# The last output projection as three rounded products, and the last expert loaded in smaller pieces

## The reference, cut to what matters

```python
mixed = jnp.concatenate([o_gla, o_att], axis=-1)     # o_gla and o_att end in a per-column gain
h = h + mixed @ w_out[l]                             # (256,1024) @ (1024,1024)
h = h + hier_moe(rms_norm_2(h, norm2_gain[l]), w_group[l], b_group[l], w_expert[l], b_expert[l],
                 w_gate[l], w_up[l], w_down[l])
return rms_norm_2(h, final_gain)
```

## Time and profile before

| | |
|---|---|
| median of 3 runs | 1330.17 us (1329.52 to 1331.28) |
| the profiled execution | 1329.42 us, its span 1327.6 us |
| PE busy | 966.9 us, 73% of the span |
| DVE, ACT, POOL busy | 451.8, 281.9, 41.8 us |
| mean DMA rate over the span | 350 GB/s, 464.45 MB |

### The profile page before, as it was taken

One profiled execution on the slowest core, in us unless ns is written; L12 is line 12 of the kernel. 1 busy time (PEld: TensorE's weight loads), 2 busy tenths in 40 slices (PEclk: granted clock), 3 DMA queues, 4 the chain that ended last, 5 costly groups with the idle time before them and its releaser, 6 DMA issues.

```text
span 1327.6 us, 30597 instructions
## 1 busy us (share of the span) xinstructions
PE 966.9 (73%) x13784; PEld 668.0 (50%) x13784; DVE 451.8 (34%) x1013; ACT 281.9 (21%) x632; POOL 41.8 (3%) x38
## 2 busy tenths in 40 slices
PE   9999999999999876466475746647574664757474
PEld 6998778888866433233243423324342432434242
DVE  4798776788844221111010211101021111102121
ACT  5655343738332100000000010000000000000001
POOL 0000201011120000000000000000000000000000
PEclk9999999999999988788787878878797978879798
DMA  9562455235494999999999999999999999999996
GB/s 329 164 246 82 150 190 190 99 112 203 175 429 177 400 433 431 427 430 433 428 431 438 429 429 435 428 429 431 436 430 434 431 429 428 431 433 432 429 426 270
DMA packets 56023, 464.45 MB, mean 350 GB/s; under 512 B 6250, under 2 KB 15268, under 8 KB 37924
## 3 DMA queue, kind: packets, MB, share of 16 engines
q1 hardware_dynamic: 55040, 460.81, 83.5%
q10 hardware_dynamic: 932, 2.92, 0.6%
HBM read 462.67 MB, written 1.05 MB: 349 GB/s over the span
## 4 chain that ended last, share of the span: by engine, by line
DMA 47%; PE 43%; DVE 6%; ACT 1%; issue 1%; SPq 1%; POOL 0%; POOLq 0%; DVEq 0%; ACTq 0%
DMA second_set<-in_w_up 41%; PE bank L2234 15%; PE bank L2877 9%; DMA ring<-in_w_up 5%; PE bank L2786 5%; PE bank L2769 3%; PE bank L2188 3%; PE bank L2212 2%; DVE ring_lo L1380 1%; PE bank L2282 1%; PE bank L2391 1%; PE bank L2299 1%; PE bank L2416 1%; DVE expert_area L2040 1%; DVE qk L1351 1%
## 5 line engine op out<-in xcount | busy, mean ns | idle before, releaser
L2890 PE MATMUL bank<-consts 128*32 128x32 f32 x52 | 8.0, 247 | 237.9 <-DMA second_set<-in_w_up 170.7
L2234 PE MATMUL bank<-ring_lo,xt_hi 128*128 128x512 f32 (+3 forms) x544 | 171.9, 383 | 0.2 <-DVE ring_lo L1380 0.2
L2786 PE MATMUL bank<-ring,consts 128*32 128x256 f32 x1952 | 118.7, 382 | 69.7 <-DVE consts L2043 41.0
L1266 ACT ACTIVATE expert_area<-bank 128x128 f32<-128x128 f32 x64 | 15.0, 275 | 656.4 <-PE bank L2877 577.6
L2040 DVE TENSOR_TENSOR expert_area<-expert_area,bank 128x128 f32<-128x128 f32 x64 | 22.9, 358 | 340.0 <-ACT expert_area L1266 340.0
L2890 PEld LDWEIGHTS bank<-consts 128*32 128x32 f32 x52 | 4.7, 138 | 245.9 <-DMA second_set<-in_w_up 176.9
L2786 PEld LDWEIGHTS bank<-ring,consts 128*32 128x32 f32 x1952 | 62.7, 109 | 121.8 <-issue 59.9
L2877 PE MATMUL bank<-second_set,expert_area 64*32 64x256 f32 x3328 | 119.4, 452 | 1.1 <-issue 1.1
L2877 PE MATMUL bank<-ring,expert_area 64*32 64x256 f32 x3328 | 118.8, 452 | 0.0
L2234 PEld LDWEIGHTS bank<-ring_lo,xt_hi 128*128 128x128 f32 x544 | 99.1, 188 | 18.4 <-issue 1.5
L2877 PEld LDWEIGHTS bank<-second_set,expert_area 64*32 64x32 f32 x3328 | 70.5, 127 | 44.6 <-issue 26.9
(11 more groups left out here) (351 smaller groups left out, 1400.5 us busy)
## 6 DMA issues: line engine op xcount, KB each, us to landing
ring<-in_w_down SPq DMA_DIRECT2D x60, 2048.0 KB, 22.1
ring<-in_w_gate SPq DMA_DIRECT2D x13, 4096.0 KB, 31.6
ring<-in_w_up SPq DMA_DIRECT2D x13, 4096.0 KB, 40.7
second_set<-in_w_gate SPq DMA_DIRECT2D x13, 4096.0 KB, 32.4
second_set<-in_w_up SPq DMA_DIRECT2D x13, 4096.0 KB, 41.7
ring<-in_w_gate SPq DMA_DIRECT2D x7, 2048.0 KB, 17.7
ring<-in_w_up SPq DMA_DIRECT2D x6, 2048.0 KB, 22.1
ring<-in_moba_w_kv SPq DMA_DIRECT2D x4, 2048.0 KB, 8.4
```

The lines of the kernel that those rows point to most:

```text
L2234: last = nc.tensor.matmul(dst, x[at], w[:, c, :], start=(piece == 0 and c == 0 and w is hi and x is x_hi), stop=(piece == 1 and c == per - ...
L2786: last = nc.tensor.matmul(down_in[SLOTS * j:SLOTS * j + SLOTS, :], turned[:, SLOTS * k:SLOTS * k + SLOTS], w[k][:, 256 * j:256 * j + 256], ...
```

## The change

For the last projection: w_out_2 becomes a split product as the others are, with its gain folded into both weight parts, and its jobs run by column blocks, (block 0, tile 0), (block 0, tile 1), (block 1, tile 0), (block 1, tile 1). The rounded parts of the two weight blocks use ring slots 5 and 1, so the loads of expert 1's down matrix (slot 5) and expert 0's up matrix (slot 1) move behind the projection's block 0 and block 1. The first quarter of `load_late_down` moves ahead of block 1's end and waits for the first tile's router product. For the last expert: gate and up matrix are both loaded in halves of the contraction, alternating, and the down matrix in three pieces (rows 0 and 1, row 2, row 3 of every four); ten bf16 products on an idle bank are issued between the halves. For the final gain: 4 KB are loaded to one partition, and TensorE spreads them by two products with ones.

```diff
-                               ("w_in_2", 5, 0), ("w_out_2", 2, 1)):
+                               ("w_in_2", 5, 0), ("w_out_2", 2, 0)):
-SPLIT = [n for n, block in enumerate(BLOCKS) if block[0] != "w_out_2"]
+SPLIT = list(range(len(BLOCKS)))
+                           "ring5", "ring1")))            # HI_AREA of the two w_out_2 blocks
+WEIGHT_GAIN = {"w_in_2": GAIN_N1, "w_out_2": GAIN_MIX}
...
# SP, load_last_expert
-                sp.dma_start(gate_up[:, 0], src).then_inc(last_landed[0], 16)
...
+                    for k, name in enumerate(("w_gate_2", "w_up_2")):      # for half in range(2)
+                        sp.dma_start(gate_up[:, k, at], src[:, at]).then_inc(last_gate_up_landed[half], 16)
...
+                for n, ks in enumerate(LAST_DOWN):                         # ((0, 1), (2,), (3,))
+                    at = slice(D * ks[0], D * (ks[-1] + 1))
+                    sp.dma_start(ring[:, 5, at], src[:, at]).then_inc(last_down_landed[n], 16)
# SP, load_late_down
+                if n == 0:
+                    sp.wait_ge(logits_in_psum, 1)
# SP, load_first_experts
                 projected("w_in_2", 3)
                 gate_or_up("w_gate_2", 0, ring[:, 0, :], first_gate_up_landed[0])
-                down(1, ring[:, 5, :], first_down_landed[1])
                 projected("w_in_2", 4)
-                gate_or_up("w_up_2", 0, ring[:, 1, :], first_gate_up_landed[0])
                 down(0, ring[:, 2, :], first_down_landed[0])
...
                 projected("w_out_2", 0)
+                down(1, ring[:, 5, :], first_down_landed[1])
                 gate_or_up("w_gate_2", 2, ring[:, 3, :], first_gate_up_landed[2])
+                load_late_down(0)
                 projected("w_out_2", 1)
+                gate_or_up("w_up_2", 0, ring[:, 1, :], first_gate_up_landed[0])
                 gate_or_up("w_up_2", 2, ring[:, 4, :], first_gate_up_landed[2])
# ACT
+            split_whole(block_of(("w_out_2", 0, 0)))        # ahead of the last gate's silu
...
             softmax_groups()
-            act.wait_ge(gla_gated, 2)
+            stream_hi("mixed", 0)
+            head_squares(PAIRS_G + 1)
+            stream_hi("mixed", 1)
+            split_whole(block_of(("w_out_2", 1, 0)))
...
-            load_row(final_row, t["final_gain_2"], row_landed)
+            act.dma_start(final_gain, t["final_gain_2"].rearrange("(a n) -> a n", a=1)).then_inc(row_landed, 16)
# DVE
+            split_lo(first_out, (0,))
+            attention_groups({1: (first_out_lo(0),), 2: (first_out_lo(1),), 3: (first_out_lo(2),),
+                              4: (first_out_lo(3),), 5: (gla_variance,), 7: (lambda: group_out(0),)})
...
-            drain_xt(GAIN_MIX, [0])
+            mix_lo(0)                                       # x_lo = turned - x_hi, into mixed_lo
...
             add_output(0, 0)
+            split_lo(second_out)
+            take_stream(0, 0)
+            add_output(1, 0)
             add_output(0, 1)
-            take_stream(0)
-            take_stream(1)
+            take_stream(0, 1)
             ask_norm2(0)
-            add_output(1, 0)
+            take_stream(1, 0)
             choose(0)
-            take_stream(0)
             add_output(1, 1)
-            take_stream(1)
+            take_stream(1, 1)
             ask_norm2(1)
...
+                        dve.wait_ge(row_in_psum, i + 1)     # last_round, after drain_down(n, i), i = 0, 1
+                        nc.vector.tensor_copy(final_row[:, 512 * i:512 * i + 512], idle_bank[:]).then_inc(row_ready, 1)
# PE
+            for half in range(2):
+                pe.wait_ge(tr_in_sbuf, TR["mixed"] + half + 1)
+                project_piece(("w_out_2", 0, 0), half)
+                if half == 0:
+                    mixed_g_transposed(1)
+            for half in range(2):
+                pe.wait_ge(tr_in_sbuf, TR["mixed"] + 2 + half + 1)
+                project_piece(("w_out_2", 0, 1), half)
+            stream_transposed(0, 0)
+            project_piece(("w_out_2", 1, 0), 0)
             pe.wait_ge(router_scaled, 1)
+            router(0, range(4))
+            project_piece(("w_out_2", 1, 0), 1)
+            project_piece(("w_out_2", 1, 1), 0, (0,))
+            stream_transposed(0, 1)
+            stream_transposed(1, 0)
+            project_piece(("w_out_2", 1, 1), 0, (1, 2))
+            router(0, range(4, KD))
+            project_piece(("w_out_2", 1, 1), 0, (3,))
...
+            project_piece(("w_out_2", 1, 1), 1)
             router(1, range(4))
             stream_transposed(1, 1)
+            rank_first()
...
+            def spread_row(half):
+                nc.tensor.matmul(idle_bank[:], const("ones")[0:1, :], final_gain[:, 512 * half:512 * half + 512],
+                                 start=True, stop=True).then_inc(row_in_psum, 1)
+            def stay_awake(n):
+                pairs = consts[:, 0:2 * P].bitcast(BF16)
+                for _ in range(n):
+                    nc.tensor.matmul(idle_bank[:], pairs[:, 0:P], pairs, start=True, stop=True)
...
                 for half in range(2):
-                    pe.wait_ge(last_landed[half], 16 * (2 - half))
+                    pe.wait_ge(last_gate_up_landed[half], 32)
                     gate_and_up(i, ring[:, 2:4, :], range(4 * half, 4 * half + 4))
+                    if half == 0:
+                        stay_awake(10)
```

More of the change, by code:

```diff
@@ L1381, in split_lo @@
                     else:
+                        first_gain = WEIGHT_GAIN[BLOCKS[b][0]] + 4 * piece
                         for c in chunks:
[L1383 removed]
+                            gain = gain_cols[:, first_gain + c:first_gain + c + 1]
                             at = slice(n * c, n * c + n)
@@ L1388, in split_lo, with mix_lo @@
                         last.then_inc(split_ready, 1)
-            def drain_xt(gains=None, tiles=range(TILES)):
-                for tile in tiles:
-                    for half in range(2):
-                        g = None if gains is None else gain_cols[:, gains + 4 * half:gains + 4 * half + 4]
-                        drain(xt[:, 4 * half:4 * half + 4, tile * P:tile * P + P], g)
+            def mix_lo(tile):
+                for half in range(2):
+                    n = tr[0]
+                    dve.wait_ge(x_hi_drained, 16 + 2 * tile + half + 1)
+                    chunks = slice(4 * half, 4 * half + 4)
+                    dst = mixed_lo[:, tile, 512 * half:512 * half + 512].rearrange("p (c s) -> p c s", s=P)
+                    nc.vector.tensor_tensor(dst, tr_bank[n % 2][:].rearrange("p (c s) -> p c s", s=P),
+                                            xt_hi[:, chunks, tile * P:tile * P + P].bitcast(F32),
+                                            ALU.subtract).then_inc(tr_in_sbuf, 1)
+                    tr[0] += 1
             def turned_lo(i):
@@ L1933, in add_output, with take_stream @@
                     proj_in_sbuf, 1)
-            def take_stream(half):
-                drain(xt[:, 4 * half:4 * half + 4, 0:P])
+            def take_stream(tile, half):
+                dst = xt[:, :, 0:P] if tile else first_stream
+                drain(dst[:, 4 * half:4 * half + 4, :])
             def ask_norm2(tile):
@@ L2193, in transpose_rows @@
                 transposes([src[:, tile, P * c:P * c + P] for c in range(4 * half, 4 * half + 4)])
-            landed = set()
-            def project(job, between=()):
-                n = JOB[job]
-                name, part, tile = job
-                b = block_of(job)
-                _, kc, _, width = BLOCKS[b]
-                w = ring[:, slot_of(b), 0:kc * width].rearrange("p (c n) -> p c n", c=kc)
-                if b not in landed:
-                    landed.add(b)
-                    pe.wait_ge(block_landed[b % FRONT], 16 * (b // FRONT + 1))
-                if n >= 2:
-                    pe.wait_ge(proj_in_sbuf, n - 1)
-                for c in range(kc):
-                    if c in between:
-                        between[c]()
-                    last = nc.tensor.matmul(proj_bank[n % 2][:, 0:width], xt[:, c, tile * P:tile * P + P],
-                                            w[:, c, :], start=(c == 0), stop=(c == kc - 1))
-                last.then_inc(proj_in_psum, 1)
             def project_piece(job, piece, chunks=range(4)):
@@ L2232, in project_piece @@
                     at = (slice(None), per * piece + c, slice(tile * P, tile * P + P))
-                    for x, w in ((x_hi, hi), (x_hi, lo), (x_lo, hi)):
-                        last = nc.tensor.matmul(dst, x[at], w[:, c, :], start=(piece == 0 and c == 0 and w is hi and
-                                                                               x is x_hi),
-                                                stop=(piece == 1 and c == per - 1 and x is x_lo))
+                    if job[0] == "w_out_2":
+                        whole_lo = mixed_lo[:, tile, P * (per * piece + c):P * (per * piece + c) + P]
+                    else:
+                        whole_lo = x_lo[at]
```

(3 more changed lines are left out.)

79 lines of the change are left out of this document (40 added, 39 removed).

## The result

| | time | profiled execution, span |
|---|---|---|
| before | 1330.54 us (1329.52 to 1331.32, 20 runs) | 1329.42, 1327.6 us |
| changed | 1334.35 us (1328.75 to 1338.47, 20 runs) | 1334.72, 1332.9 us |

The ratio is 1.0028, 95% interval 1.0018 to 1.0038: slower by 0.3%, where 0.5% faster was forecast. The spread alone is news: 9.7 us between the changed kernel's executions, 1.8 us before. In its profiled execution the changed kernel is ahead by 4.0 us when expert 0 starts and by 2.05 at the first load that TensorE waits for in the full stream (474.38 for 476.43). It is behind by 3.98 when expert 61 starts (1285.17 for 1281.19), so 6.0 us are lost between these two, nearly all in the loop over expert pairs. The end takes 1.6 more.

The account below looks back on a forecast made before the run. TensorE was taken to bound the projection, whose end sets the start of the gap-free weight stream. Stream -4.9, gain row -1.2 and last expert -0.55 summed to -6.65 us: 1323.5 against 1330.17, range 1321.2 to 1327.4.

Parts of the forecast that it names:

- no engine's work inside that stretch can move the end: Gap-free expert-weight stream: its start, the bytes left by the rate, and what follows the last byte set the end.
- a late up matrix (D): Rival: expert 0's up matrix, moved back in SP's queue, lands late; +4.05 us, 1334.2, chance 0.04.
- The projection's products: Last projection on TensorE: rounded products at 0.232 us each make 27.5 us into 22.2, 5.3 us less.
- The stage: From the last projection to the router's second half: gives 4.9 us, so expert 0 starts at 425.1.
- The wait for `choose(0)`: End of the stage: the last job's add queues behind it on DVE, holding TensorE about 0.5 us.
- The stream: Expert-weight loads: gap-free part reached earlier, -4.9 us, bounds 0 and -5.6.
- The stream has no gap from 414.6 on: Loads ahead of expert 0: SP's new order keeps data flowing without a break from 414.6 us.
- the backlog: Loads still owed at the stream's start: alone would set the gap-free start at 426.5, the -5.6 us bound.
- rival C: Another chain (DVE's block 1 split, or the logits) takes TensorE's place; only -1.75 us left, 1328.4, chance 0.08.
- The gain row: Final gain: 512 KB load leaves the full stream, 4 KB stay; -1.2 us, bounds 0 and -1.4.
- The pieces: Last expert's weights in alternating halves and down pieces, with filler products: -0.55 us, bounds -0.8 and +1.5.
- Rival B: Last expert: clock falls between the halves, tail costs up to 1.5 us and not -0.55; 1325.6, chance 0.12.

Follow-up runs that it names:

- e12: Changed kernel with 8 more TensorE instructions (16 satisfied waits) ahead of the loop over expert pairs; 1325.62 us, ratio 0.9960.
- e3: Kernel before with the changed projection alone (old last expert and gain row), plus 64 added TensorE instructions ahead of the loop; 1328.04 us, ratio 0.9982.
- e1: Changed kernel with 64 more TensorE instructions (128 satisfied waits) ahead of the loop over expert pairs; 1325.77 us, ratio 0.9967.
- e11: Kernel before with only the last expert's alternating halves, ten filler products and three down pieces; gain row loaded as before; 1329.75 us, ratio 0.9994.
- e2: Kernel before with 68 more TensorE instructions (136 satisfied waits), so its loop starts where the changed kernel has it; 1338.81 us, ratio 1.0057.
- e5: Changed kernel with 256 more TensorE instructions (512 satisfied waits) ahead of the loop; 1342.12 us, ratio 1.0098.
- e14: Changed kernel with 188 more TensorE instructions (376 satisfied waits), loop at the same place in a block as before the change; 1326.77 us, ratio 0.9977.
- e13: e12 without the ten filler products between the last expert's halves; 1325.89 us, ratio 0.9962.
- e7: e1 without the ten filler products between the last expert's halves; 1326.67 us, ratio 0.9974.

## Why the prediction was wrong

**The step that failed** is in its first paragraph: "no engine's work inside that stretch can move the end". It holds while TensorE has slack: in the kernel before it waits in most rounds 3.6 to 5.9 us for the first weight set and 12.3 to 13.9 for the second. A round with stalls takes TensorE 12 us longer (3.04, 5.71, 2.69 and 0.82 in the one shown) and up to 18. Even where a wait for a load is left over (3.33 us in the one shown), slots come free later in the round and the next loads are issued later (890.84 for 879.82, 1010.10 for 996.00). By the starts of the second set's products three such rounds cost 1.5 us each and the fourth, with the round behind it, 2.7; 1.2 us of it come back by expert 61. I had counted every instruction of the change for its duration and none for its place. No rival had the mechanism; the 4% for slower stood on a late up matrix (D), and no trace shows it: expert 0 waits for no load. Price: the ratios 1.0028 and 0.9960 of the changed kernel and of e12 are 9 us apart.

**The projection's products**: right. 0.2325 us each against 0.232, and no stall for either of block 1's pieces. By the Trainium skill's four passes (FP8 and Floating Point Precision, TensorE Precision Notes) one pass would be a quarter of the 0.859 us fp32 chunk, an estimate of 0.215; this trace keeps to the row.

**The stage**: -4.0 in this execution, and -4.5 for -4.9 when its late front is taken off. The first product starts at 387.72 and not 387.1; 0.47 of this is the delay that was there at 100 us. The rest is that the product gains nothing by needing one half only: it starts 2.06 us behind the first turn of the input (385.66), where the kernel before took 2.04 (385.20 to 387.24), as `mixed_lo` on DVE now stands between. From the first product to expert 0 it takes 38.27 us where the prediction's times have 38.0. The add on DVE at 406.96 stands in the chain, but TensorE did three products beside it and idled 0.08 us. The wait for `choose(0)` was foreseen with 0.5 us and is 0.49.

**The stream**: the term that was mis-sized most among those seen, -4.9 forecast and -2.0 measured by e3. "The stream has no gap from 414.6 on" failed: 0.81 MB in 414 to 418. The lead in bytes at 440 us is 2.7 to 3.1 us in e3 and e1, and e3 ended 2.0 us ahead. The prediction had named the backlog as what would set it, at -5.6; it set it at about half. This is rival C's outcome in part, but not its chain: DVE's split held up nothing and the late quarter was issued as soon as the logits were there (411.05). The stream does not lose the 0.7 us between: e3 is still 1.17 MB ahead at 1240 us. But the loads that TensorE waits for land only 1.8 us ahead, from 474.61 (for 476.43) to 1243.94 (for 1245.70), so the bytes overstate the lead. Why they do is not settled.

**The gain row**: -1.2 predicted, -1.4 measured. **The pieces**: -0.55 predicted, -0.5 measured by e11, which is not told from none, so the agreement is in part luck. The prediction has two errors here: the filler takes 2.33 us and not 1.2, since a product is 512 columns wide (0.23 us each), and it is hidden only while TensorE waits for loads. Rival B (the clock falls between the halves) shows in no profile with the filler, and without it in one of two.

**The sum by measured terms**: -2.0 - 1.4 - 0.5 = -3.9; e1 has -4.2 and e12 -4.6. Instead of 1323.5 the change, at a good place, gives 1325.6, inside the forecast range; as it stands, 1334.35.

## What to carry to other kernels

In a kernel with a long hardware loop, count the instructions of the loop and of all that stands ahead of it on that engine. If the loop comes close to filling seven blocks of 256, as this one of 1583 does, any edit ahead of it can cost more than it brings; look at the instruction queue's packets and at the idle time put down to "issue" before judging an edit, and try it at a second place before discarding it. When a stage is shortened ahead of a full stream, reckon the gain by when the first load that is waited for inside the stream lands, not by the start of the engine that opens the stream; the bytes moved by a fixed moment come nearer, but were 0.9 us too good in e3.

## What the runs showed of the hardware

- A TensorE loop of 1583 instructions runs 13 rounds with 6 or 7 instruction packets when it lies in seven blocks of 256, and with 34 to 42 when it needs eight with more than a few instructions in the last: 41 to 79 us of stalls (added waits taken off), and about 9 us of time in the two kernels where few waits or none were added (the changed one against e12, e2 against the kernel before). Eight blocks are 2048 instructions, which is the buffer's size by the Trainium skill (Runtime: NRT & Kernel Launch, Instruction fetch mechanics); that a loop must leave a block free is how the runs look, not something they prove, as no loop of another length was run. Why only some rounds and, at place 211, only some executions are struck stays open.
- A satisfied wait took TensorE 0.05 us (25.34 us for 512 in e5, 18.0 for 376 in e14, each one record in the timeline as idle time on issue).
- In e13 TensorE was idle for 3.13 us before the second halves with its clock granted at 1.00, and the clock fell to 0.50 at about 1309.4 us, over 1 us after work had begun again. In e7, behind 2.53 us of idle time, it did not fall. In the changed kernel it fell at about 1296.5 us, at work, behind idle times of 1.15 and 1.07 us.
